# Attention scans: where VectorE takes the sums of weights and their reciprocals in a unit

## The chip, the core and the metric

The kernel runs on one core of a Trainium2 chip. The metric is the device time of one execution in microseconds (us). Five engines work side by side: PE (TensorE, with its weight loads listed apart as PEld), DVE (VectorE), ACT (ScalarE), POOL (GpSimd) and SP (SyncE, which here only issues transfers). Each executes its own list of instructions in order; they meet on semaphores.

## The reference, cut to what matters

The program is two transformer blocks one behind the other. The second has two attention branches, and those hold the change. Both have 8 query heads of width 64 over 2 key/value heads; 1024 rows of queries are worked in 8 blocks of 128. The window branch lets a query block see its own block of keys, the two beside it and 256 context keys; the grid branch lets it see all 1024 keys and the 256 context keys:

```python
def grid_attention(q, k, v, kc, vc):
    b, L, hq, dh = q.shape
    nb = L // BLK
    k_all = jnp.concatenate([k, kc], axis=1)
    v_all = jnp.concatenate([v, vc], axis=1)
    qb = jnp.moveaxis(q.reshape(b, nb, BLK, hq, dh), 1, 0)
    ob = lax.map(lambda qi: dense_attention(qi, k_all, v_all, None), qb)
    return jnp.moveaxis(ob, 0, 1).reshape(b, L, hq * dh)
```

For each row of queries this is: scores, their maximum m, the weights exp(score - m), the sum of the weights, weights times values, and that divided by the sum. The window branch puts a "sink" logit into the maximum and the sum.

## The kernel before, in words

**Tiling.** The class `AttGroup` holds one key/value head of one branch with its 4 query heads; there are four of them, run one after the other: at10 and at11 (window branch), at20 and at21 (grid branch). After the projections of a group comes its scan. A scan has 16 units; a unit is one block n of 128 queries and two heads x0 and x0+1 (`self.units`, n from 0 to 7, x0 0 and 2).

**What one unit takes.** PE multiplies queries and keys into PSUM banks 0 to 3 (`scores`: two pieces a head in the window branch, three in the grid branch). DVE takes the maximum of each piece, joins them and negates (`scores` in `dve`, "neg"; in the window branch it first adds the masks `wm` to the bank). ACT makes the exponentials of a head (tile P) and their sum per piece into columns 4 to 6 of the small tile `sm` (`soft` in `act`). DVE adds the three columns into column 8 and takes the reciprocal there (`soft` in `dve`: one "sum" and one "rs" a head). PE transposes P by blocks of 128 keys, two blocks of both heads into one bank, 4 or 5 alternating (`turn`; called a block pair below: 2 or 3 of them a unit in the window branch, 5 in the grid branch). ACT copies the bank into Ph, DVE subtracts to get the rest Pl (`turn` in `dve`), PE multiplies values by Ph and Pl into bank 6 (`av`). Ahead of the first product of a unit PE spreads the two reciprocals of column 8 over bank 6 with two matmuls each (`bank<-cst,at20sm`). At the end (`fin`) ACT copies half of bank 6 to `rsx`, DVE adds the halves and multiplies by the reciprocals into `y`.

**What sets the order.** Every engine walks the same list, `walk`, and does its own part of each step. Step j of unit u does the block pair j of u (`turn`), two steps later its product (`av`), behind the last one `fin`; and between them it does the steps of the next unit, from `first`:

```python
if self.win:
    return [lambda: scores(n, x0), lambda: scores(n, x0 + 1), lambda: soft(n, x0), lambda: soft(n, x0 + 1)]
return [lambda: scores(n, x0), None, lambda: soft(n, x0), lambda: scores(n, x0 + 1), None, lambda: soft(n, x0 + 1)]
```

So in the grid branch DVE's list within one unit is, with a dash for the next unit's work: Pl of pair 0, -maxima of head x0, Pl of pairs 1 and 2, -sum and reciprocal of head x0, Pl of pair 3, -maxima of head x0+1, Pl of pair 4, -sum and reciprocal of head x0+1, `fin`. In the window branch: Pl 0, -maxima x0, Pl 1, -maxima x0+1, Pl 2, -both sums and reciprocals, `fin`. For the very first unit of a scan, `first` runs without a unit ahead of it. PE also has matmuls of another product in its list, `bank<-h,wslot`, the gate of the branch, one of its 8 steps at a time at fixed steps of units 0 to 11 (grid) or 0 to 13 (window) (`gate_pe`); ACT copies each finished gate tile out to `sq` at the end of every second unit (`gate_act`).

Waits go by semaphores that count up; a wait that an engine has already passed is not issued again (`Eng.wait_ge`).

## Time and profile before

| | us |
|---|---|
| median of 3 runs | 4696.1 (4693.6 to 4708.62) |
| the profiled execution | 4691.44, its span 4689.6 |
| scan of at10, first to last sum | 2802.8 to 2933.1 of the span |
| scan of at11 | 3000.7 to 3131.1 |
| scan of at20 | 3289.4 to 3479.0 |
| scan of at21 | 3573.9 to 3762.2 |

The profile gives the busy time of each engine and, for every instruction, start, duration and what ended the idle time ahead of it. The chain of waits is followed back from the last instruction of the program: what stands in it is what sets the time. The four scans take about 640 of the 4690 us; nothing outside them is touched. Line numbers in the rows are those of helpers: L193 and L196 are PE's matmul and transpose, L202 ACT's activation, L205 DVE's and POOL's tensor_tensor, L208 tensor_scalar, L223 the maximum, L226 the sum, L217 the reciprocal. Tiles tell the instructions apart.

### The profile page before, as it was taken

The numbers are of one execution on the slowest core, as the hardware profiler recorded it, in microseconds if no ns is written. First come the engines' busy times: TensorE is split into PE (matmuls) and PEld (weight loads), VectorE is DVE, ScalarE is ACT, GpSimd is POOL, SyncE is SP. The second block draws the span as 40 slices with busy tenths as digits, with TensorE's granted clock in tenths as the row PEclk, the third lists the DMA queues.
The fourth block names the chain that finished last, engine by engine and source line by source line (L and its number), as shares of the span: only waits on it lengthen the run. The fifth ranks groups of instructions, "written<-read, shape, count | busy, mean of one in ns | idle before, by whom it ended". The sixth has DMA issues, their size and how long they took to land.

```text
span 4689.6 us, 46418 instructions
## 1 busy us (share of the span) xinstructions
PE 4275.1 (91%) x18566; PEld 3109.3 (66%) x18566; DVE 2383.8 (51%) x3800; ACT 1547.6 (33%) x2988; POOL 903.6 (19%) x695
## 2 busy tenths in 40 slices
PE   7896889998999999988889999989888998999997
PEld 3455754757788888645457866565665677888886
DVE  2778864153556663336362337564667754333334
ACT  3465631122211111332332215352554633222222
POOL 2112224121334441016161000001000021000001
PEclk9998899999999999897979999999999999999999
DMA  5112243112333441211111211021000031111111
GB/s 193 41 61 86 77 132 110 32 45 81 90 108 113 121 117 48 107 55 45 54 45 54 77 35 39 17 66 47 24 25 19 19 117 36 54 45 53 42 41 63
DMA packets 257800, 308.90 MB, mean 66 GB/s; under 512 B 19072, under 2 KB 209936, under 8 KB 256304
## 3 DMA queue, kind: packets, MB, share of 16 engines
q1 hardware_dynamic: 238096, 227.15, 15.8%
q0 software_dynamic: 17408, 75.64, 5.2%
q8 instruction: 146, 2.39, 0.2%
q10 hardware_dynamic: 2080, 3.15, 0.2%
q14 instruction: 70, 0.57, 0.0%
HBM read 271.61 MB, written 34.28 MB: 65 GB/s over the span
## 4 chain that ended last, share of the span: by engine, by line
PE 61%; DVE 10%; ACT 5%; issue 1%; POOL 1%; DMA 1%; POOLq 0%; DVEq 0%; ACTq 0%
PE bank L193 60%; PE bank L196 2%; DVE Mx L205 1%; ACT Mx L202 1%; ACT at21P L202 1%; ACT at20P L202 1%; POOL sq L205 1%; DVE at21sm L223 1%; DVE at20sm L223 1%; DVE x L211 0%; DMA wslot<-in_w_in 0%; DVE wfl L205 0%; DVE at11sm L223 0%; DVE at21Pl L205 0%; DVE at10sm L223 0%
## 5 line engine op out<-in xcount | busy, mean ns | idle before, releaser
L193 PE MATMUL bank<-h,wslot 128*128 128x512 f32 (+2 forms) x1616 | 691.5, 566 | 32.9 <-DMA wslot<-in_w_in 19.1
L193 PE MATMUL bank<-hT,wslot 128*128 128x512 f32 (+3 forms) x1136 | 462.4, 564 | 17.1 <-DVE hT L211 7.3
L193 PEld LDWEIGHTS bank<-h,wslot 128*128 128x128 f32 (+1 forms) x1616 | 292.0, 191 | 262.7 <-issue 245.6
L193 PEld LDWEIGHTS bank<-hT,wslot 128*128 128x128 f32 (+1 forms) x1136 | 212.4, 190 | 242.8 <-issue 237.8
L193 PE MATMUL bank<-ffn1h,wfh 128*128 128x512 f32 x704 | 279.8, 397 | 11.7 <-DVE ffn1l L211 10.9
L211 DVE SCALAR_TENSOR_TENSOR x<-bank,mod,x 128x512 f32<-128x512 f32 x224 | 164.4, 746 | 245.1 <-PE bank L193 244.8
L193 PE MATMUL bank<-ffn2h,wgh 128*128 128x512 f32 x704 | 276.5, 393 | 9.7 <-DVE ffn2l L211 9.2
L193 PE MATMUL bank<-ffn1l,wfh 128*128 128x512 f32 x704 | 275.0, 391 | 0.0
L193 PE MATMUL bank<-ffn2l,wgh 128*128 128x512 f32 x704 | 274.9, 390 | 0.0
L193 PE MATMUL bank<-ffn2h,wgl 128*128 128x512 f32 x704 | 274.7, 390 | 0.0
L193 PE MATMUL bank<-ffn1h,wfl 128*128 128x512 f32 x704 | 274.5, 390 | 0.0
L205 DVE TENSOR_TENSOR wfl<-wslot,wfh 128x1024 fp32r<-128x1024 f32 (+2 forms) x92 | 152.6, 1659 | 148.3 <-ACT wfh L202 148.3
L205 POOL TENSOR_TENSOR ffn2al<-ffn2ga,ffn2ah 128x512 fp32r<-128x512 f32 x44 | 57.4, 1304 | 655.3 <-ACT ffn2ah L202 655.3
L226 DVE TENSOR_REDUCE at2a<-ffn1t 128x128 f32<-128x1024 f32 x72 | 143.1, 1988 | 45.6 <-POOL ffn1t L205 45.6
L205 POOL TENSOR_TENSOR sq<-sq 128x512 f32<-128x512 f32 (+1 forms) x77 | 94.8, 1231 | 362.9 <-ACT sq L202 358.7
L193 PEld LDWEIGHTS bank<-ffn1h,wfh 128*128 128x128 f32 x704 | 132.6, 188 | 44.5 <-DVE ffn1l L211 10.6
L193 PEld LDWEIGHTS bank<-ffn2h,wgh 128*128 128x128 f32 x704 | 132.6, 188 | 43.2 <-DVE ffn2l L211 10.2
L211 DVE SCALAR_TENSOR_TENSOR ffn2ga<-ffn2gw,par,ffn2ga 128x1024 f32<-128x1024 f32 x44 | 56.5, 1285 | 199.6 <-ACT ffn2ga L202 198.8
L193 PEld LDWEIGHTS bank<-ffn2h,wgl 128*128 128x128 f32 x704 | 132.8, 189 | 27.7
L193 PEld LDWEIGHTS bank<-ffn1h,wfl 128*128 128x128 f32 x704 | 132.6, 188 | 27.9
L193 PEld LDWEIGHTS bank<-ffn2l,wgh 128*128 128x128 f32 x704 | 132.8, 189 | 26.7
L193 PEld LDWEIGHTS bank<-ffn1l,wfh 128*128 128x128 f32 x704 | 132.8, 189 | 25.4
(573 smaller groups left out, 9502.7 us busy)
## 6 DMA issues: line engine op xcount, KB each, us to landing
wslot<-in_w_in SPq DMA_DIRECT2D x40, 1024.0 KB, 5.7
ffn1t<-in_w_mod POOLq DMA_DIRECT2D x64, 512.0 KB, 4.9
wslot<-in_w_ffn_in SPq DMA_DIRECT2D x44, 512.0 KB, 5.4
Mx<-acsT SPq DMA_DIRECT2D x32, 512.0 KB, 4.9
at1w<-in_ada_w POOLq DMA_DIRECT2D x24, 512.0 KB, 4.7
wslot<-in_ffn_w_gate SPq DMA_DIRECT2D x22, 512.0 KB, 4.0
wslot<-in_ffn_w_up SPq DMA_DIRECT2D x22, 512.0 KB, 5.3
wslot<-in_w_ffn_out SPq DMA_DIRECT2D x20, 512.0 KB, 5.3
```

What stands on the lines that cost most here:

```text
L193: return Counted() if counting[0] else self.q.matmul(o, l, r, start=start, stop=stop)
L196: return Counted() if counting[0] else self.q.transpose(o, i, ident)
L202: return Counted() if counting[0] else self.q.activation(o, i, f, **k)
L205: return Counted() if counting[0] else self.q.tensor_tensor(o, a, b, op)
L211: return Counted() if counting[0] else self.q.scalar_tensor_tensor(o, a, s, b, op0, op1)
L223: return Counted() if counting[0] else self.q.reduce_max(o, a, AX.X)
L226: return Counted() if counting[0] else self.q.reduce_sum(o, a, AX.X)
```

## The change

`soft` in `dve` is taken out of the walk (it becomes a step that does nothing), and a new function `sums(u)` does both heads of a unit at once. It is called from `turn`, behind the Pl of pair 0 of the same unit: that is one step later than before for every unit but the first, on the other side of the `fin` of the unit ahead. Both sums stand first, then both reciprocals.

```diff
-            def soft(n, x):
-                s_ = self.sm[n, x]
-                e.wait_ge(*st.act.after("p", n, x))
-                e.reduce_sum(s_[:, 8:9], s_[:, 4:7]).then_inc(d("sum", n, x), 1)
-                e.wait_ge(*d.now())
-                e.reciprocal(s_[:, 8:9], s_[:, 8:9]).then_inc(d("rs", n, x), 1)
+            def sums(u):
+
+                n, x0 = u
+                for x in (x0, x0 + 1):
+                    s_ = self.sm[n, x]
+                    e.wait_ge(*st.act.after("p", n, x))
+                    e.reduce_sum(s_[:, 8:9], s_[:, 4:7]).then_inc(d("sum", n, x), 1)
+                for x in (x0, x0 + 1):
+                    s_ = self.sm[n, x]
+                    e.wait_ge(*d.after("sum", n, x))
+                    e.reciprocal(s_[:, 8:9], s_[:, 8:9]).then_inc(d("rs", n, x), 1)
...
                 self.bt.give((u, i), d.now())
+                if i == 0:
+                    sums(u)
...
-            self.walk(scores, soft, turn, lambda u, i: None, fin, lambda i, j: None)
+            self.walk(scores, lambda n, x: None, turn, lambda u, i: None, fin, lambda i, j: None)
```

DVE's list in the scan of at20, one unit from the middle. Pl is the rest of a block pair, sm0 and sm1 the small tiles of the two heads of the coming unit, sm2 that of the unit behind it. Before, from the Pl of pair 2 on:

```order
L205 TENSOR_TENSOR at20Pl1<-bank5,at20Ph1 128x512
L226 TENSOR_REDUCE at20sm0<-at20sm0 128x1
L217 RECIPROCAL at20sm0<-at20sm0 128x1
L205 TENSOR_TENSOR at20Pl2<-bank4,at20Ph2 128x512
L223 TENSOR_REDUCE at20sm1<-bank3 128x1
L223 TENSOR_REDUCE at20sm1<-bank0 128x1
L223 TENSOR_REDUCE at20sm1<-bank1 128x1
L208 TENSOR_SCALAR at20sm1<-at20sm1 128x1 x2
L205 TENSOR_TENSOR at20Pl3<-bank5,at20Ph3 128x512
L226 TENSOR_REDUCE at20sm1<-at20sm1 128x1
L217 RECIPROCAL at20sm1<-at20sm1 128x1
L205 TENSOR_TENSOR rsx<-bank6,rsx 64x256
```

After, from the Pl of pair 4 of the same unit on:

```order
L205 TENSOR_TENSOR at20Pl3<-bank5,at20Ph3 128x512
L205 TENSOR_TENSOR rsx<-bank6,rsx 64x256
L205 TENSOR_TENSOR y2<-rsx,bank6 64x128 x2
L205 TENSOR_TENSOR at20Pl0<-bank4,at20Ph0 128x512
L226 TENSOR_REDUCE at20sm0<-at20sm0 128x1
L226 TENSOR_REDUCE at20sm1<-at20sm1 128x1
L217 RECIPROCAL at20sm0<-at20sm0 128x1
L217 RECIPROCAL at20sm1<-at20sm1 128x1
L223 TENSOR_REDUCE at20sm2<-bank2 128x1
```

The four small instructions have left the places behind Pl of pair 2 and of pair 4, and stand between Pl of pair 0 of the next unit and the first maximum of the unit behind that.

DVE's list in the scan of at10, the difference at one unit (- is before, + is after; wm is the mask, added to the bank ahead of its maximum):

```order
-L226 TENSOR_REDUCE at10sm4<-at10sm4 128x1
-L217 RECIPROCAL at10sm4<-at10sm4 128x1
-L226 TENSOR_REDUCE at10sm5<-at10sm5 128x1
-L217 RECIPROCAL at10sm5<-at10sm5 128x1
 L205 TENSOR_TENSOR rsx<-bank6,rsx 64x256
 L205 TENSOR_TENSOR y1<-rsx,bank6 64x128 x2
 L205 TENSOR_TENSOR at10Pl0<-bank4,at10Ph0 128x512
+L226 TENSOR_REDUCE at10sm4<-at10sm4 128x1
+L226 TENSOR_REDUCE at10sm5<-at10sm5 128x1
+L217 RECIPROCAL at10sm4<-at10sm4 128x1
+L217 RECIPROCAL at10sm5<-at10sm5 128x1
```

Here they move from ahead of `fin` to behind the first Pl. The lists of PE, ACT, POOL and SP keep their order.

## Rows read from the trace of the kernel before

**Rows 1.** The page, chain that ended last, shares of the span by engine.

```profile
PE 61%; DVE 10%; ACT 5%; issue 1%; POOL 1%; DMA 1%; POOLq 0%; DVEq 0%; ACTq 0%
```

**Rows 2.** Stretches, at10 and at20: us, busy PE PEld DVE ACT POOL, clock, DMA, GB/s.

```profile
2795.00:2940.00 145.00, 123.91 (x617) 84.31 (x617) 103.29 (x342) 75.35 (x231) 0.00 (x0) 0.94 0.11 33
...
3275.00:3490.00 215.00, 182.48 (x997) 136.72 (x995) 144.62 (x358) 118.04 (x298) 1.26 (x1) 0.93 0.07 22
```

**Rows 3.** Waits, 3275 to 3490: who for whom, us in total, times, longest.

```profile
DVE at20sm L226 <- ACT at20P L202: 38.2, 32, 3.3
```

**Rows 4.** Instructions of L226 and L217: duration ns min/median/max, first and last start.

```profile
L226 DVE TENSOR_REDUCE at20sm<-at20sm x32: 155/156/158, 3289.4 to 3479.0; 128x1 f32<-128x3 f32 x32
```

```profile
L217 DVE RECIPROCAL at20sm<-at20sm x32: 162/163/166, 3289.6 to 3479.2; 128x1 f32<-128x1 f32 x32
```

**Rows 5.** Timeline, grid branch, around a first head's sum: start us, us, engine.

```profile
3391.00 0.60 ACT L202 ACTIVATE at20Ph<-bank 128x512 fp32r<-128x512 f32 x1
...
3391.15 0.16 DVE L226 TENSOR_REDUCE at20sm<-at20sm 128x1 f32<-128x3 f32 x1 [0.77 <-ACT at20P L202]
...
3391.34 0.16 DVE L217 RECIPROCAL at20sm<-at20sm 128x1 f32<-128x1 f32 x1
...
3391.64 0.69 DVE L205 TENSOR_TENSOR at20Pl<-bank,at20Ph 128x512 fp32r<-128x512 f32 x1
```

**Rows 6.** Timeline, window branch, behind a second head's sum, up to `fin`.

```profile
2885.86 0.38 ACT L202 ACTIVATE rsx<-bank 64x256 f32<-64x256 f32 x1
...
2886.06 0.16 DVE L217 RECIPROCAL at10sm<-at10sm 128x1 f32<-128x1 f32 x1
...
2886.28 0.42 DVE L205 TENSOR_TENSOR rsx<-bank,rsx 64x256 f32<-64x256 f32 x1
```

**Rows 7.** Timeline, opening of the scan of at20, PE and DVE.

```profile
3289.51 0.42 PE L193 MATMUL bank<-at20kl,at20qs 128*128 128x256 f32 x1
3289.58 0.16 DVE L217 RECIPROCAL at20sm<-at20sm 128x1 f32<-128x1 f32 x1
3289.66 1.60 DVE L223 TENSOR_REDUCE at20sm<-bank 128x1 f32<-128x512 f32 x3
```

**Rows 8.** Chain of waits, window branch, two units: start us, us, what.

```profile
2887.53 0.69 DVE at10Pl L205
...
2892.70 1.12 ACT at10P L202 x4
2893.96 0.63 PE bank L196 x4
...
2903.78 0.69 DVE at10Pl L205
```

**Rows 9.** Timeline, window branch, PE at the transposes that the chain passes by.

```profile
2885.95 0.14 PEld L196 LDWEIGHTS bank<-cst,at10P 128*128 128x128 f32 x1 [0.35 <-ACT at10P L202]
2886.26 0.60 PE L196 MATMUL bank<-cst,at10P 128*128 128x128 f32 x4
```

**Rows 10.** Chain of waits, grid branch, from a Pl of pair 0 on.

```profile
3398.29 0.69 DVE at20Pl L205
...
3401.66 0.66 PE bank L196 x4
```

**Rows 11.** Timeline, grid branch, the other unit: its "neg" and ACT's exponentials.

```profile
3388.72 0.46 DVE L208 TENSOR_SCALAR at20sm<-at20sm 128x1 f32<-128x1 f32 x2
...
3389.22 0.68 ACT L202 ACTIVATE at20P<-bank,at20sm 128x512 f32<-128x512 f32 x1
```

**Rows 12.** Timeline, grid branch, PE behind the load of gate weights in mid-scan.

```profile
3349.72 1.97 PE L193 MATMUL bank<-h,wslot 128*128 128x512 f32 x2 [4.39 <-DMA wslot<-in_w_in]
```

**Rows 13.** Timeline, window branch, last unit of the scan of at10.

```profile
2934.74 0.69 DVE L205 TENSOR_TENSOR at10Pl<-bank,at10Ph 128x512 fp32r<-128x512 f32 x1 [0.23 <-ACT at10Ph L202]
2934.86 1.12 PE L193 MATMUL bank<-cst,at10sm 128*64 128x128 f32 x4
```

**Rows 14.** A stretch of at20 behind the gate's units; columns as in rows 2.

```profile
3455.90:3461.00 5.10, 5.10 (x26) 4.38 (x26) 4.52 (x13) 2.32 (x5) 0.00 (x0) 0.69 0.00 0
```

## The prediction

> **What bounds the kernel now.** I read the chain of waits first, by engine [rows 1]: PE holds 61% of the span, DVE 10%, ACT 5%. The change touches nothing but DVE's list in the four attention scans, about 640 of 4690 us, so I then read the stretches of those scans [rows 2]. PE is busy 124 of 145 us in one and 182 of 215 in the other, at a mean granted clock of 0.94 and 0.93; DVE 103 and 145 us. No engine is full: a scan is a loop of dependences that passes from engine to engine, and the question is which DVE instructions stand in that loop. The waits [rows 3] make the change look worth a lot: in one grid scan DVE stands 38.2 us in front of the sums, 32 times, until ACT has written the last exponentials. But a wait counts only where what stands behind it on DVE could have gone earlier.
>
> **Part 1: what is taken away from behind the maxima.** 32 sums of 0.155 us and 32 reciprocals of 0.163 us a scan [rows 4], 64 pairs in the window scans and 64 in the grid scans. Take the first head of a grid unit [rows 5]: sum at 3391.15, reciprocal 0.19 later at 3391.34, over at 3391.50. Behind it stands the Pl of pair 3, and that needs ACT's Ph, which stands behind the same exponentials on ACT: 3391.00 to 3391.60. Pl starts at 3391.64, by the Ph and not by the reciprocal. Worth nothing, and the wait in front of the sum only changes its name: DVE will now stand as long in front of Pl. The second head is the same with `fin` behind it [rows 6]: ACT's copy `rsx` stands behind the exponentials and ends at 2886.24, the reciprocal at 2886.22, the add starts at 2886.28. Worth 0.02 us at most. Where the odd unit has ACT copy a gate tile first, the copy comes later still and the cover is wider. So the removal gives 0 in steady state, and the cover is ACT's own next instruction.
>
> One place is different: the opening of a grid scan, where no unit runs ahead. There the sum of the first head holds back the maxima of the second: they start at 3289.66, 0.08 after the reciprocal at 3289.58, all three in 1.60 us [rows 7]. Without it the first of them could run while ACT works, and the other two as PE delivers: its last score matmul runs from 3289.51 to 3289.93, so the second piece is there by 3289.51. Second and third maximum, 768 of the 1280 columns and so three fifths of the 1.60, 0.96 us, would end near 3290.5, where the three ended at 3291.26: 0.7 us earlier. The first transposes wait for this, so **-0.7 us in each of two grid scans, -1.4**. The window scans do both maxima ahead of the sums already: 0.
>
> **Part 2: what is put in behind the first Pl.** Four small instructions between Pl of pair 0 and the next maximum. No wait comes with them in front of the sums (the transposes of pair 0 needed both heads' exponentials already); each reciprocal waits for its sum. The price of one place: a DVE instruction that needs nothing starts 0.08 after the start of a small one ahead of it (reciprocal 3289.58, maximum 3289.66 [rows 7]); one that needs the result of its predecessor starts 0.19 after it [rows 5]. So sum, sum at 0.08, reciprocal at 0.19, reciprocal at 0.27, next maximum at 0.35: **0.35 us**. Bounds: four times 0.07 to 0.08 is 0.3 if nothing had to be waited for; the sum of the durations, 2 x 0.155 + 2 x 0.163 = 0.64, if nothing overlapped. I take 0.35, since both spacings are read from these very instructions.
>
> The Trainium skill, page "VectorE: DVE Perf Modes", section "The DRAIN you can't avoid", says that the next operation does not start until the pipeline is empty. The maximum that starts 0.08 after the start of a reciprocal of 0.16 [rows 7] speaks against it; by that rule a place costs 0.64. It is a rival below.
>
> **Part 3: how many of these places stand in the loop.** *Window branch.* The chain goes Pl of pair 0 (2887.53), masks, maxima, Pl 1, masks, maxima, ACT's exponentials (2892.70), transposes of the next unit (2893.96) [rows 8], then stays on PE through the whole next unit, and comes back to a Pl of pair 0 at 2903.78. So every second place is on it in full: 7 of 16, and the last one ahead of the unit without gate steps too, 8 x 0.35 = 2.8 us a scan. In the unit that the chain passes by, PE's first weight load waits for ACT at 2885.95, its transposes start at 2886.26 behind the gate product [rows 9]; a load leads its matmul by 0.03 where nothing is queued, so there is 0.28 of slack and a place costs 0.35 - 0.28 = 0.07: 5 times, 0.35 us. Two places are free: behind the opening, where the chain runs on PE, and ahead of the load of gate weights in mid-scan. Last, the final unit: PE's spread of the reciprocals starts at 2934.86, right behind the `fin` of the unit ahead, while Pl of pair 0 runs 2934.74 to 2935.43 [rows 13]. Now the reciprocals come only behind that Pl. A free instruction follows a large one about 0.09 before its end: sums from 2935.34, second reciprocal from 2935.61, over at 2935.77. With no maxima and no gate product in front of it PE waits for it: first spread at about 2935.7 instead of 2934.86, **+0.84**. A window scan: 2.8 + 0.35 + 0.84 = 4.0, two of them 8.0 us.
>
> *Grid branch.* The loop is two units again. In the one the chain goes Pl of pair 0 (3398.29), maxima, "neg", Pl of pair 1, transposes of pair 3 (3401.66) [rows 10], since these need the bank that Pl 1 frees: in full. In the other the chain comes over PE and ACT to the exponentials of the first head at 3389.22, but DVE's "neg" for them is over at 3388.72 + 0.46 = 3389.18 [rows 11], and 0.04 is what a semaphore takes here (Pl 0.04 behind Ph in [rows 5]): slack 0, in full too. Of 15 places (the last unit has no maxima behind it) one is hidden in the opening, and one where PE stands 4.39 us for gate weights [rows 12], during which DVE catches up. 13 x 0.35 = 4.55 a scan, 9.1 us for two. In the last grid unit PE's spread comes behind transposes that wait for Pl of pair 0 anyway: 0.
>
> **Sum.** 8.0 + 9.1 - 1.4 = **+15.7 us**. The profiled execution took 4691.4 (span 4689.6), which would become 4707.1; the median of the three runs is 4696.1, 4.7 above it, and I predict for the median: 4711.8. With a place at 0.3 the 42 full ones (16 window, 26 grid) give 12.6, the ten half-hidden ones 0.2, the two window ends some 1.5, less 1.4: +12.9. At 0.64 it is 26.9 + 3.6 + 2.3 - 1.4 = +31.4.
>
> **Rivals.**
> *A good part of the places is covered.* "Slack 0" in one kind of grid unit rests on two instants 0.04 apart, and a shift of Ph against "neg" that the first delay itself brings could free the second. If those 6 places a grid scan fall out (12 x 0.35 = 4.2), and the half-hidden ones and the window ends too (0.7 + 1.7), +9.1 is left: 4705.2. For it: bounds that close tend to hide a little slack between them. Against: DVE's start in that unit follows PE, so both shift together.
> *No overlap on DVE.* The place costs 0.64: +31.4, 4727.5. Against it the 0.08 [rows 7]; for it that no row shows two sums or two reciprocals in a row. This is the rule of the Trainium skill named above.
> *The clock.* PE idles 0.35 us more per unit. Behind the gate's units the granted clock is 0.69 over 5.1 us [rows 14], a part of it at the lower of the two levels (1.2 against 2.4 GHz), right behind waits of PE for Pl and for P. 5.1 us at 0.69 instead of 1.00 is 1.6 us lost; three such more a scan are +19, in all 4731. The gate product, which keeps PE busy in 12 or 14 units of 16, speaks against it.
> *Faster.* The removed pairs cost DVE 0.27 each (0.19 + 0.08), 0.54 a unit. If the release of Pl 3 and of `fin` were by DVE and not by ACT, and the four instructions found room behind Pl 0 because "neg" were early, the about 60 units would give back 0.54 each, -32 us: 4664. This decides itself at one point: whether the reciprocal ends behind ACT's copy. It ends 0.10 before Ph [rows 5] and 0.02 before `rsx` [rows 6], so I see it only where ACT is quicker than shown.
>
> **How the numbers follow.** Chance of the forecast 0.62, of the covered places 0.20, of no overlap 0.08, of the clock 0.06, of faster 0.04. A difference of under 0.3%, 14.1 us, can hardly be told from none here, and the forecast stands just over it: of its 0.62 I put 0.38 above and 0.24 below. Slower 0.38 + 0.08 + 0.06 = 0.52, within 0.3% 0.24 + 0.20 = 0.44, faster 0.04. The range: the forecast by the bounds of the place is +12.9 to +31.4, the covered places give +9; with some 2 us either way for the runs it is 4701 to 4728.
>
> **What would show it.** Right: behind each first Pl four small rows 0.08, 0.19 and 0.27 after the first, the maximum at 0.35; the waits in front of L226 gone, waits of Pl for Ph and of `fin` for `rsx` longer by about as much, no less time between exponentials and Pl 3; a pair of grid units 0.7 us longer, a pair of window units 0.42 longer than 16.25 [rows 8]; PE waiting for DVE's reciprocals once at the end of a window scan; second maxima of the grid opening 0.7 us earlier. Wrong: a pair of grid units longer by 0.35 only, or the small rows 0.16 apart, or a lower clock in the loop.

## The result, and the profile after

The changed kernel takes 4712.79 us (median of 10 runs, 4707.69 to 4717.64) against 4692.66 us for the kernel before (10 runs, 4689.92 to 4708.62). The ratio is 1.0042, with a 95% interval of 1.0033 to 1.0051: slower by 15.5 to 24 us, 20.1 between the medians. The prediction said +15.7 us and 4711.8. Of the two, +15.7 is the one to judge: that 4711.8 lies within 1 us of the measured 4712.79 is luck, since the base of 4696.1 was the median of three runs and 3.4 above that of ten, and the change was forecast 4.4 too small. One run in eleven of the version "grid branch only" below took 8666.03 us; it is left out of every comparison.

The page of the changed kernel, busy time by engine (us, share of the span, instructions), and then the chain that ended last, by engine:

```profile
PE 4284.3 (91%) x18566; PEld 3111.7 (66%) x18566; DVE 2368.0 (50%) x3800; ACT 1550.5 (33%) x2988; POOL 906.7 (19%) x695
...
PE 58%; DVE 12%; ACT 5%; POOL 2%; issue 1%; DMA 1%; POOLq 0%; DVEq 0%; ACTq 0%; SPq 0%
```

Against [rows 1] the chain has passed from PE (61% to 58%) to DVE (10% to 12%). These shares say only in which direction to look. The stretches of the scans of at10 and at20, with the columns of [rows 2] (length, busy PE, PEld, DVE, ACT, POOL, granted clock, DMA, GB/s):

```profile
2799.00:2951.00 152.00, 127.91 (x618) 85.53 (x617) 100.20 (x344) 76.27 (x231) 0.00 (x0) 0.93 0.10 32
...
3300.00:3514.00 214.00, 183.08 (x999) 137.99 (x1000) 134.78 (x353) 116.99 (x295) 0.00 (x0) 0.93 0.07 22
```

The windows are not cut at the same instants as in [rows 2], so their lengths are not to be compared, and the one of before holds a few more DVE instructions of the preparation. DVE's busy time has fallen from 144.6 to 134.8 us in the grid scan, about half of it by these few and the other half because small instructions that stood in separate pairs now overlap (32 sums and 32 reciprocals of about 0.16 alone are 10.2 us, 16 places of 0.32 are 5.1). So the busy time falls while the time rises: what costs here is the order, not the amount of work. To compare lengths I take an anchor that exists in every kernel, from the first maximum of a scan to its last `y`. In the profiled executions that is 140.1, 139.0, 206.5 and 205.3 us for at10, at11, at20 and at21 before, together 690.9; after, 145.6, 143.8, 210.6 and 208.8, together 708.9. So **18.0 us came in inside the four scans**. The two profiled executions are 26.2 us apart (the one of after, at 4717.64, is the longest of its ten). Of that, 5.3 lie ahead of the first scan, where no instruction has moved, 2.2 between at10 and at11, and 0.7 behind the last. The 5.3 say nothing about the change: in a second profile of the kernel before the first scan starts at 2792.3 us, in the first at 2798.9. The 2.2 are taken up below.

Where does DVE wait now? The waits in the scan of at20, columns as in [rows 3] (who for whom, us in total, times, longest):

```profile
DVE at20Pl L205 <- ACT at20Ph L202: 37.0, 28, 4.7
DVE rsx L205 <- ACT rsx L202: 32.3, 16, 2.3
```

The same two rows of the kernel before, over the stretch of [rows 3]:

```profile
DVE at20Pl L205 <- ACT at20Ph L202: 15.1, 15, 4.9
...
DVE rsx L205 <- ACT rsx L202: 6.3, 13, 1.0
```

The 38.2 us in front of L226 [rows 3] have no row any more. In their place the waits of Pl for Ph grew by 21.9 and those of `fin` for `rsx` by 26.0, together 47.9. Removing the largest wait of DVE bought nothing: it took another name and grew by what the small instructions no longer filled. The small instructions are all still there, 32 of each a scan.

Now the place itself. Timeline of the changed kernel in the scan of at20 (start us, us, engine, what; in brackets the wait ahead of it). A row with x2 or x3 is a group of instructions and its time is from the start of the first to the end of the last:

```profile
3455.81 0.69 DVE L205 TENSOR_TENSOR at20Pl<-bank,at20Ph 128x512 fp32r<-128x512 f32 x1 [0.47 <-ACT at20Ph L202]
...
3456.42 0.21 DVE L226 TENSOR_REDUCE at20sm<-at20sm 128x1 f32<-128x3 f32 x2
3456.60 0.23 DVE L217 RECIPROCAL at20sm<-at20sm 128x1 f32<-128x1 f32 x2
3456.74 1.60 DVE L223 TENSOR_REDUCE at20sm<-bank 128x1 f32<-128x512 f32 x3
...
3458.88 0.69 ACT L202 ACTIVATE at20P<-bank,at20sm 128x512 f32<-128x512 f32 x1 [0.20 <-DVE at20sm L208]
```

Pl, then the first sum at 0, the first reciprocal at 0.18, the maximum at 0.32. From the lengths of the x2 groups (0.21 for two of 0.146, 0.23 for two of 0.156) the second sum stands at 0.07 and the second reciprocal at 0.07 to 0.08 behind the first. The last row is what makes it expensive: ACT had been idle for 0.20 us before the exponentials and was let go by DVE's "neg", in the very kind of unit in which the prediction called the slack 0.

What a place costs, in each of the two kinds of unit, shows best in the times of `y`. First the kernel before, then the one after, three successive units in the scan of at20 (the timeline of DVE):

```profile
3421.53 0.59 DVE L205 TENSOR_TENSOR y<-rsx,bank 64x128 f32<-64x128 f32 x2
...
3433.14 0.59 DVE L205 TENSOR_TENSOR y<-rsx,bank 64x128 f32<-64x128 f32 x2
...
3445.40 0.59 DVE L205 TENSOR_TENSOR y<-rsx,bank 64x128 f32<-64x128 f32 x2
```

```profile
3430.23 0.59 DVE L205 TENSOR_TENSOR y<-rsx,bank 64x128 f32<-64x128 f32 x2
...
3442.81 0.59 DVE L205 TENSOR_TENSOR y<-rsx,bank 64x128 f32<-64x128 f32 x2
...
3454.75 0.59 DVE L205 TENSOR_TENSOR y<-rsx,bank 64x128 f32<-64x128 f32 x2
```

Before, steps of 11.61 and 12.26; after, 11.94 (3442.81 to 3454.75) and 12.58. **Each kind of unit is 0.32 to 0.33 longer, the full price of a place in both.** The window branch, three units in the scan of at10, before and then after:

```profile
2878.94 0.59 DVE L205 TENSOR_TENSOR y<-rsx,bank 64x128 f32<-64x128 f32 x2
...
2886.73 0.59 DVE L205 TENSOR_TENSOR y<-rsx,bank 64x128 f32<-64x128 f32 x2
2887.53 0.69 DVE L205 TENSOR_TENSOR at10Pl<-bank,at10Ph 128x512 fp32r<-128x512 f32 x1 [0.21 <-ACT at10Ph L202]
...
2895.19 0.59 DVE L205 TENSOR_TENSOR y<-rsx,bank 64x128 f32<-64x128 f32 x2
```

```profile
2886.77 0.59 DVE L205 TENSOR_TENSOR y<-rsx,bank 64x128 f32<-64x128 f32 x2
...
2894.88 0.59 DVE L205 TENSOR_TENSOR y<-rsx,bank 64x128 f32<-64x128 f32 x2
2895.50 0.69 DVE L205 TENSOR_TENSOR at10Pl<-bank,at10Ph 128x512 fp32r<-128x512 f32 x1
...
2903.47 0.59 DVE L205 TENSOR_TENSOR y<-rsx,bank 64x128 f32<-64x128 f32 x2
```

Steps of 7.79 and 8.46 became 8.11 and 8.59: +0.32 in the one kind of unit, +0.13 to 0.14 in the other. The rows of Pl show where the other 0.18 went: before, DVE stood idle for 0.21 us between `y` and Pl of pair 0, waiting for Ph; after, Pl follows the end of `y` in 0.03.

The end of a window scan is the place where PE meets the reciprocals. Timeline of the changed kernel in the last unit of at10, to be read against [rows 13]:

```profile
2944.08 0.69 DVE L205 TENSOR_TENSOR at10Pl<-bank,at10Ph 128x512 fp32r<-128x512 f32 x1
...
2944.69 0.21 DVE L226 TENSOR_REDUCE at10sm<-at10sm 128x1 f32<-128x3 f32 x2
2944.87 0.23 DVE L217 RECIPROCAL at10sm<-at10sm 128x1 f32<-128x1 f32 x2
...
2945.18 1.08 PE L193 MATMUL bank<-cst,at10sm 128*64 128x128 f32 x4 [1.40 <-DVE at10sm L217]
```

PE's spread of the reciprocals began 0.12 us behind the start of Pl of pair 0 in [rows 13]. Now it begins 1.10 behind it, with a named wait of 1.40 us for L217. One unit earlier the same wait stands once more, with 0.95 us, but that step (7.02 to 7.34) grew by no more than in the kernel of the section "The place alone", where PE does not wait for reciprocals.

And the opening of the grid scan, PE and DVE, against [rows 7]:

```profile
3303.79 0.68 DVE L223 TENSOR_REDUCE at20sm<-bank 128x1 f32<-128x512 f32 x1
...
3307.33 0.41 PE L193 MATMUL bank<-at20kl,at20qs 128*128 128x256 f32 x1
3307.36 1.02 DVE L223 TENSOR_REDUCE at20sm<-bank 128x1 f32<-128x512 f32 x2 [2.89 <-PE bank L193]
```

The first maximum of the second head now runs 3.6 us ahead of the other two, and these start with PE's last score matmul and take 1.02 instead of 1.60. First maximum to first Pl is 11.12 and 10.62 us in the two grid scans, where it was 11.80 and 11.81. The 0.7 is the one gain of the change, and it is as predicted. The other 0.5 of the second scan does not repeat (a second profile of the changed kernel has 11.12 twice) and goes with a higher granted clock: 0.80 from the first maximum to the first `y`, 0.71 in the kernel before.

### The profile page after: what moved, and what is told of

It reads as the page before. It is cut to its first block, busy times and chain, and to the rows that moved or that the text cites. A ratio compares the mean times of both kernels' runs of the same rounds, so it can differ in the third digit from the quotient of the medians.

```text
span 4715.8 us, 46424 instructions
## 1 busy us (share of the span) xinstructions
PE 4284.3 (91%) x18566; PEld 3111.7 (66%) x18566; DVE 2368.0 (50%) x3800; ACT 1550.5 (33%) x2988; POOL 906.7 (19%) x695
## 3 DMA queue, kind: packets, MB, share of 16 engines
q1 hardware_dynamic: 238096, 227.15, 15.7%
## 4 chain that ended last, share of the span: by engine, by line
PE 58%; DVE 12%; ACT 5%; POOL 2%; issue 1%; DMA 1%; POOLq 0%; DVEq 0%; ACTq 0%; SPq 0%
PE bank L193 57%; PE bank L196 1%; DVE Mx L205 1%; ACT at21P L202 1%; ACT at20P L202 1%; DVE at20sm L223 1%; DVE at21sm L223 1%; ACT Mx L202 1%; POOL sq L205 1%; DVE y L205 0%; DVE x L211 0%; DVE at11sm L223 0%; DVE wfl L205 0%; DMA wslot<-in_w_in 0%; DVE at10sm L223 0%
## 5 line engine op out<-in xcount | busy, mean ns | idle before, releaser
L193 PE MATMUL bank<-ffn1h,wfh 128*128 128x512 f32 x704 | 279.9, 398 | 11.7 <-DVE ffn1l L211 10.8
L193 PE MATMUL bank<-ffn2h,wgh 128*128 128x512 f32 x704 | 276.2, 392 | 10.2 <-DVE ffn2l L211 9.6
L226 DVE TENSOR_REDUCE at2a<-ffn1t 128x128 f32<-128x1024 f32 x72 | 143.1, 1987 | 47.7 <-POOL ffn1t L205 47.7
L193 PEld LDWEIGHTS bank<-ffn2h,wgh 128*128 128x128 f32 x704 | 132.4, 188 | 43.9 <-DVE ffn2l L211 10.8
```

Source lines behind the costliest of these rows:

```text
L193: return Counted() if counting[0] else self.q.matmul(o, l, r, start=start, stop=stop)
L226: return Counted() if counting[0] else self.q.reduce_sum(o, a, AX.X)
```

## The experiments

Two theories stood against each other after the result. **The place:** the 18 us come from the four small instructions behind Pl of pair 0, whatever they compute, and nothing came back for their leaving. **The late results:** they come from sums and reciprocals being ready later, for PE. Beside these: is the place 0.33 because of overlap on DVE, and why 20 us rather than 15.7? Each version's median is compared with that of the kernel before timed beside it: 4695.85 for the first four below, 4694.22 for the next four, 4694.41 for the last two. "Scans" is the sum of the four lengths as above, from one profile. A ratio is not the quotient of the two medians; the two can differ by some 3 us.

### Without sums and reciprocals

Leaves out the division by the sum of the weights: PE spreads the column of the negated maximum instead of that of the reciprocal, and DVE does neither sums nor reciprocals.

```diff
-                        e.wait_ge(*st.dve.after("rs", n, x0 + x))
-                        e.matmul(..., self.sm[n, x0 + x][:, 8:9].to_broadcast([128, 64]), ident)...
+                        e.wait_ge(*st.dve.after("neg", n, x0 + x))
+                        e.matmul(..., self.sm[n, x0 + x][:, 3:4].to_broadcast([128, 64]), ident)...
...
-            self.walk(scores, soft, turn, ...)
+            self.walk(scores, lambda n, x: None, turn, ...)
```

> Takes all 128 sums of weights and 128 reciprocals out of the four scans and puts nothing in their place; PE spreads the column with the negated maximum instead of the reciprocal, so the scans leave the division by the sum out. Theory 'the place' (the removed pairs stood behind ACT's next instruction and were worth nothing; what costs is where the four instructions now stand): the kernel before less only the 0.7 us of each grid opening, -1 to -2 us. Rival 'the pairs were on the path': they were worth up to 0.54 us a unit, -10 to -32 us, and the new place costs that much more.

Measured 4689.55 us against 4695.85, ratio 0.9994 (0.9985 to 1.0003): between 7 us less and 1.4 us more, so the medians' -6.3 stands at the edge of it. Scans 692.3 against 690.9, and all steps of the loop are as before (12.26 and 11.60, 8.45 and 7.79). The cover is seen in the timeline of this kernel, ACT and DVE around the place where a first head's sum used to be:

```profile
3407.26 0.60 ACT L202 ACTIVATE at20Ph<-bank 128x512 fp32r<-128x512 f32 x1
...
3407.90 0.69 DVE L205 TENSOR_TENSOR at20Pl<-bank,at20Ph 128x512 fp32r<-128x512 f32 x1 [1.26 <-ACT at20Ph L202]
```

Ph starts, and 0.64 behind that start comes Pl, exactly as in [rows 5] (3391.00 and 3391.64) where sum and reciprocal stood between. Taking the pairs away altogether, the most that any move out of this position can give, is worth nothing in the steps; a gain of 10 us or more is excluded. That is Part 1 of the prediction, shown by its removal. What remains, -0.7 in each grid opening, was here too: first maximum to first Pl 11.11 and 11.12.

### The place alone

The kernel before with four spare instructions of the same size behind Pl of pair 0, whose result nobody reads:

```diff
+            def spare(u):
+                n, x0 = u
+                for x in (x0, x0 + 1):
+                    e.reduce_sum(self.sm[n, x][:, 9:10], self.sm[n, x][:, 4:7]).then_inc(d("sum9", n, x), 1)
+                for x in (x0, x0 + 1):
+                    e.wait_ge(*d.after("sum9", n, x))
+                    e.reciprocal(self.sm[n, x][:, 9:10], self.sm[n, x][:, 9:10]).then_inc(d("rs9", n, x), 1)
...
+                if i == 0:
+                    spare(u)
```

> The kernel before, with its sums and reciprocals where they were, and two more sums and two more reciprocals into an unused column of the small tile, at the place where the change puts them (behind Pl of pair 0). Theory 'the place': the same loss as the change less its gain at the grid openings and without the late reciprocals at the window ends (1.2 us each): about 20 + 1.4 - 2.4, +19 us. Rival 'late results': if what costs is that PE gets the reciprocals late, these spare instructions, for which nobody waits, cost clearly less than the change, under +10.

4709.82 us, ratio 1.0035 (1.0021 to 1.0048): +14.0 between the medians, +17.3 in the scans, where +19 was expected and under +10 by the rival. Scans 708.2, where after has 708.9. That the two sums are so close is partly chance: the window scans are 285.4 us here and 289.4 there, the grid scans 422.8 and 419.5. The steps are the better witness. The steps are those of the changed kernel: `y` in at20 at

```profile
3430.17 0.59 DVE L205 TENSOR_TENSOR y<-rsx,bank 64x128 f32<-64x128 f32 x2
3442.10 0.59 DVE L205 TENSOR_TENSOR y<-rsx,bank 64x128 f32<-64x128 f32 x2
3454.68 0.59 DVE L205 TENSOR_TENSOR y<-rsx,bank 64x128 f32<-64x128 f32 x2
```

that is 11.93 and 12.58, and in the window branch 8.10 and 8.59. No result is late here, no sum has been moved, and every step of the loop has its loss. This decides between the two theories for the steady state: it is the place. What the late results add is seen at the end of a window scan only, where PE of this kernel does not wait:

```profile
2935.57 1.12 PE L193 MATMUL bank<-cst,at10sm 128*64 128x128 f32 x4
```

From the last `y` but one to the last `y` of at10 this kernel takes 4.99, the changed one 5.71, before 4.50. So the end costs 1.2 in all, 0.5 of it by the place and 0.7 by the late reciprocals. This interval too has longer forms: 5.15 in one of four of the kernel before, 6.09 and 6.11 in later versions.

### The place twice

The changed kernel with the same four spare instructions behind its own:

```diff
                 if i == 0:
                     sums(u)
+                    spare(u)
```

> The changed kernel with the four instructions of the place twice (the second time into an unused column). Theory 'the place': another 0.35 us or somewhat less at each of the 42 places in the loop, the 0.28 of slack in the ten others now used up so that they cost in full as well: 52 x 0.33 to 0.35, +17 to +18 over the changed kernel, about +37 to +38 over the one before. Rival 'slack used up only once or clock': over +25 on top of the changed kernel if longer waits of PE bring its clock down again and again.

4723.51 us, ratio 1.0064 (1.0051 to 1.0077), 13.7 above the kernel with one spare place. Scans 722.4, 13.5 above after. The steps in at20 are 12.89 and 12.25, another 0.31 in each. The window branch is the telling one, its three rows in at10:

```profile
2881.86 0.59 DVE L205 TENSOR_TENSOR y<-rsx,bank 64x128 f32<-64x128 f32 x2
2890.28 0.59 DVE L205 TENSOR_TENSOR y<-rsx,bank 64x128 f32<-64x128 f32 x2
2899.18 0.59 DVE L205 TENSOR_TENSOR y<-rsx,bank 64x128 f32<-64x128 f32 x2
```

8.42 and 8.90: the kind of unit that took the first place for 0.14 takes the second for 0.31, in full. So there was a slack, it was 0.32 - 0.14 = 0.18 us, and the first place has used it up. Slack is a thing that one delay consumes. The total came out lower than expected: +37 to +38 over the kernel before was forecast, measured are +27.7 between the medians (+24 to +36 by the ratio's interval) and +31.5 in the scans. The steps grew nearly as forecast, 13 a scan by 0.31 (0.33 to 0.35 was said), which is 4.0; but the four scans grew by 3.7, 2.9, 3.4 and 3.4 over the changed kernel. The missing part lies in the openings, the steps with the load and the ends, which come in different lengths from profile to profile (below).

### The kernel before once more

The same text as the kernel before, to see how far profiles of one program differ.

> The kernel before, once more, for a second profile of it. The changed kernel's scans measured 18.0 us longer and the stretch between the two window scans 2.2 us longer, at a granted clock of 0.96 instead of 1.00. If that 2.2 is the luck of one execution, stretches outside the scans differ by about as much between these two profiles of one and the same kernel; if it comes with the change, they agree within 0.3 us.

4695.14 us, ratio 0.9998 (0.9989 to 1.0007). Scans 691.4 against 690.9, but a single scan differs by up to 1.2 (at11 140.2 against 139.0, at20 205.5 against 206.5), so the 0.5 of the sum is a lucky figure. Steps of the loop repeat within 0.02. The last interval of the window scans was 4.44 and 5.15. Outside the scans the two profiles do differ, the start of the first scan by 6.6 us. But the stretch between the two window scans, which the expectation was about, was 59.0 both times.

### Window branch only, grid branch only

The changed kernel with the old `soft` for one branch and `sums` for the other:

```diff
+            def soft(n, x):
+                if self.win:
+                    return
...
-                if i == 0:
+                if i == 0 and self.win:
                     sums(u)
```

> The change in the two window scans alone; the grid scans keep their sums behind the maxima. Theory 'the place', by the steps measured in the changed kernel (0.32 and 0.14 us in turn, 1.2 at the end, half of it luck of the clock): 4.5 us in each window scan, +9 in all; grid scans as before, the stretch around the load of gate weights in mid-scan 17.0 us. Rival 'clock': the grid's load stretch is longer here too.

> The change in the two grid scans alone. Theory 'the place': 13 x 0.32 less 0.7 at the opening is +3.5 a scan. Theory 'clock after the load': the stretch with the load of gate weights takes 18 us or more instead of 17.0, as in five of the six grid scans with the four instructions in that place, because TensorE's clock stays at the lower level for longer; then +4.5 a scan, +9 in all. If it takes 17.0 here, the longer stretch was luck.

Window only: 4703.1 us, ratio 1.0022 (1.0012 to 1.0031), +8.9. Grid only: 4703.2 without the run of 8666.03, ratio 1.0018 (1.0009 to 1.0027), +9.0. Window only is as expected (+9), grid only lies at the +9 of the clock theory and 2 above the +7 of the other. The two together are 17.9 against the 20.1 of the whole change: within the intervals they add up, and each branch carries about half. In the traces the scans are 698.8 and 699.2, +7.9 and +8.3 over before, and each branch that kept its order kept its steps (12.27 and 11.61 in the grid branch of the first). The grid's step with the load of gate weights took 17.07 and 16.90 us in the first kernel, 16.95 and 18.06 in the second: one scan of each kind, so neither theory is decided by it.

### Serial in the place

Sum, reciprocal, sum, reciprocal, each behind its predecessor's end:

```diff
                     e.reduce_sum(s_[:, 8:9], s_[:, 4:7]).then_inc(d("sum", n, x), 1)
-                for x in (x0, x0 + 1):
-                    s_ = self.sm[n, x]
-                    e.wait_ge(*d.after("sum", n, x))
+                    e.wait_ge(*d.now())
                     e.reciprocal(s_[:, 8:9], s_[:, 8:9]).then_inc(d("rs", n, x), 1)
```

> The changed kernel with the four instructions of the place in the order sum, reciprocal, sum, reciprocal. If the price of a place is the dependence (0.18 from a sum to its reciprocal) and not the number of instructions, it now is 2 x (0.18 + 0.08) = 0.52 instead of 0.33: the steps of 11.93 us in the grid scans become 12.12, and the kernel is 52 x 0.19 = +10 us over the changed one, +30 over the one before. If four instructions cost the same in any order, the steps stay at 11.93.

4720.43 us, ratio 1.0059 (1.0046 to 1.0072): +26.2 between the medians where +30 was expected; scans 719.7, which is 10.8 above after. The place in at20:

```profile
3347.99 0.15 DVE L226 TENSOR_REDUCE at20sm<-at20sm 128x1 f32<-128x3 f32 x1
3348.17 0.16 DVE L217 RECIPROCAL at20sm<-at20sm 128x1 f32<-128x1 f32 x1
3348.25 0.14 DVE L226 TENSOR_REDUCE at20sm<-at20sm 128x1 f32<-128x3 f32 x1
3348.42 0.16 DVE L217 RECIPROCAL at20sm<-at20sm 128x1 f32<-128x1 f32 x1
3348.50 1.60 DVE L223 TENSOR_REDUCE at20sm<-bank 128x1 f32<-128x512 f32 x3
```

The rows show both spacings: a reciprocal 0.17 or 0.18 behind the start of the sum that it reads, and the next, unrelated instruction 0.08 behind the start of the reciprocal. The place is 0.51 long. All steps of the loop grow by it: 12.77 and 12.12 in the grid branch, 8.79 and 8.30 in the window branch, about 0.19 above after in each. What the prediction feared as "no overlap" is half there with the four in this order, and it costs some 10 us in the scans.

### One sum and one reciprocal for both heads

The six small tiles lie side by side in one, and one instruction takes both heads:

```diff
-            self.sm = Ring([sb(f"{nm}sm{i}", [16]) for i in range(6)])
+            self.smt = sb(f"{nm}sm", [96])
+            self.sm = Ring([self.smt[:, i * 16:i * 16 + 16] for i in range(6)])
...
+                two = self.smt[:, i * 16:i * 16 + 32].rearrange("p (x c) -> p x c", c=16)
+                e.reduce_sum(two[:, :, 8:9], two[:, :, 4:7]).then_inc(d("sum", n, x0 + 1), 1)
+                e.wait_ge(*d.now())
+                e.reciprocal(two[:, :, 8:9], two[:, :, 8:9]).then_inc(d("rs", n, x0 + 1), 1)
```

> The changed kernel with the small tiles of the two heads side by side in one tile, so that one sum (128x2 from 128x2x3) and one reciprocal do both heads: two instructions in the place instead of four. By the same spacings 0.18 + 0.08 = 0.26 instead of 0.33 a place: steps of 11.86 us in the grid, 52 x 0.07 = 3.6 us under the changed kernel, about +16 over the one before. If the price were 0.08 an instruction, it would halve to 0.16, about 9 us under the changed kernel.

4710.42 us, ratio 1.0036 (1.0023 to 1.0048): +16.2, as expected; scans 706.7, 2.2 below after. The place:

```profile
3346.95 0.15 DVE L226 TENSOR_REDUCE at20sm<-at20sm 128x2 f32<-128x6 f32 x1
3347.14 0.17 DVE L217 RECIPROCAL at20sm<-at20sm 128x2 f32<-128x2 f32 x1
3347.22 1.60 DVE L223 TENSOR_REDUCE at20sm<-bank 128x1 f32<-128x512 f32 x3
```

0.27 instead of 0.32. Half the instructions save only 0.05, because the two that went were the cheap, overlapped ones. The pair that depends on each other is what the place costs. Between 0.27 (this), 0.32 (after) and 0.51 (serial) the scans go 706.7, 708.9, 719.7. By the sum of the prediction's 52 places (42 full and ten whose slack is gone by then) serial should be 52 x 0.19 = 9.9 above after, and this 52 x 0.05 = 2.6 below; measured 10.8 and 2.2. That fits the count of the places; the steps, each longer by 0.19 in the one and shorter by 0.05 to 0.06 in the other, show it more surely, since single parts of a scan vary by 1 us and more.

### The opening only

The kernel before, with only the first unit of each grid scan late:

```diff
             def soft(n, x):
+                if not self.win and (n, x // 2 * 2) == self.units[0]:
+                    return
...
+                if i == 0 and not self.win and u == self.units[0]:
+                    sums(u)
```

> The kernel before, with only the first unit of each grid scan doing its sums behind its first Pl, where the maxima behind them are covered by PE; all other units as before. By the steps: first maximum to first Pl 11.12 instead of 11.81 us in both grid scans, all later steps as before, -1.4 us in all, 0.03%, below what the times can tell. It is the version that the steps point to. Rival: the first place costs something too, and nothing is left of the 1.4.

4692.47 us, ratio 1.0000 (0.9991 to 1.0009). First maximum to first Pl went from 11.80 and 11.81 to 10.77 and 10.63, a gain of 1.0 and 1.2 in the trace; the scans are 689.3 against 690.9. In the run times 1 or 2 us cannot be told from nothing, and part of the gain in the trace goes with the granted clock of these openings, 0.81 and 0.80 instead of 0.70 and 0.71. It is the only part of the change that the traces show to gain anything, and no version that I ran is measurably faster than the kernel before.

### The changed kernel once more

> The changed kernel once more, for a second profile and in the same call as the one above. The steps repeat within 0.02 us (11.93 and 12.58 in the grid, 8.11 and 8.60 in the window); the time is 18 to 20 us over the one before. What differs from profile to profile without a change of the kernel (openings, the stretch around the load, the ends, the stretch behind the first window scan) differs again by up to 1 to 3 us each. If the longer load stretch comes with the change, it is 18 us or so here in at least one of the two grid scans.

4716.01 us, ratio 1.0048 (1.0034 to 1.0062): +21.6, where 18 to 20 was expected; scans 709.4 against 708.9. The steps repeat (12.58 and 11.92 to 11.94, 8.60 and 8.11). The step with the load is 16.77 in at20 and 17.94 in at21.

## Why the prediction was right, step by step

**The removal is worth nothing: right.** Without the sums and reciprocals at all the kernel takes the same time (0.9985 to 1.0003), and Pl starts 0.64 behind the start of Ph with or without them.

**The opening: right up to the first Pl**, 0.7 us (11.80 to 11.12); 1.2 in the second grid scan, 0.5 of which goes with the clock. Behind the first Pl some of it is gone again (the table below).

**The price of a place: nearly right.** Predicted sums at 0 and 0.08, reciprocals at 0.19 and 0.27, the maximum at 0.35. Measured 0, 0.07, 0.18, about 0.25, 0.32 to 0.33. The sums are 0.146 us long here where they were 0.155. On 42 full places that is -1 us. The rival of no overlap (0.64) has fallen: the maximum starts 0.14 behind the start of reciprocals that together take 0.23. The Trainium skill, page "VectorE: DVE Perf Modes", section "The DRAIN you can't avoid", says in one sentence that the next operation does not start until the pipeline is empty, and at the end of the same paragraph that one that is not held starts earlier. The prediction quoted the first sentence alone. The rows here agree with the second.

**Every grid place in full: right for the steps of the loop**, and this was the weakest step of the prediction. It is not so for the step with the load and for the last one (below). The covered places, the rival with a chance of 0.20, would have left one kind of grid unit unchanged; both got 0.32 to 0.33 longer, and the second place added 0.31 to both again. The "slack 0" that was read from two instants 0.04 apart was real.

**The half-hidden window place: the size was off, because a second path was overlooked.** A step costs 0.13 to 0.14 and not 0.07. The slack of 0.28 in front of the transposes [rows 9] was there. They start 0.85 us behind the start of the gate product ahead of them before (2885.41 and 2886.26) and 0.87 behind it after (2893.26 and 2894.13), while the distance from the weight load to them shrinks from 0.31 to 0.03. But the place also delays ACT's copy `rsx`, with it `fin`, and `fin` stands ahead of the next Pl of pair 0 on DVE. There the slack is smaller: the 0.21 of idle time ahead of Pl in the rows above, less the 0.03 that is left when nothing is waited for, is 0.18, and 0.32 - 0.18 = 0.14. The same 0.18 fits the other two prices: of 0.27 (joined) 0.08 to 0.09 is paid in this kind of step, of 0.51 (serial) 0.33. Ten times 0.07 is +0.7 us. The pair of window units is 0.45 longer, where 0.42 was said.

**The end of the window scans: the mechanism was right, the size was off.** PE waits for L217, and the step comes to 1.2 and not 0.84, +0.8 in two scans. The place itself costs 0.5 there, as the kernel with spare instructions shows, and 0.3 of this is between Pl of pair 0 and Pl of pair 1 of the last unit, a place that the prediction did not count; the late reciprocals cost 0.7. PE waits at the last two units, not only at the last.

**What is left.** The account can be checked part by part. From the mean of two profiles of the changed kernel less the mean of two of the kernel before, both scans of a branch together (us):

| part | window: predicted | measured | grid: predicted | measured |
|---|---|---|---|---|
| first maximum to first `y` | 0 | +1.0 | -1.4 | -0.9 |
| places in full (16 and 26) | +5.6 | +5.2 | +9.1 | +8.5 |
| half-hidden places (10) | +0.7 | +1.5 | | |
| step with the load of gate weights | 0 | +0.2 | 0 | +1.7 |
| last step | +1.7 | +2.1 | 0 | -1.3 |
| sum | +8.0 | +10.0 | +7.7 | +8.0 |

The grid branch came out right partly because two parts that the prediction put at nothing nearly cancel. In the window branch +1.0 comes from an opening of at10 that is 13.8 to 14.0 us in seven profiles and 14.8 to 15.1 in five; the kernel without sums, which has nothing in the place, is among the five, so this is not shown to be the change's. The two grid parts go with the granted clock. In the step with the load in the middle [rows 12] the prediction said that the place is hidden. PE of the changed kernel, behind that load in at20:

```profile
3368.17 2.05 PE L193 MATMUL bank<-h,wslot 128*128 128x512 f32 x2 [4.46 <-DMA wslot<-in_w_in]
```

The wait is that of [rows 12], but what follows differs. Stretches of some 7 us behind the load, columns as above, of the kernel before, of the changed one, and of the kernel with the opening only, which has no place there at all:

```profile
3349.70:3357.00 7.30, 7.28 (x31) 4.92 (x32) 2.52 (x6) 2.88 (x8) 0.00 (x0) 0.77 0.00 1
```

```profile
3368.10:3375.50 7.40, 7.33 (x27) 5.39 (x28) 1.40 (x3) 2.99 (x8) 0.00 (x0) 0.58 0.00 1
```

```profile
3344.70:3352.00 7.30, 7.23 (x27) 5.28 (x28) 1.62 (x5) 2.99 (x8) 0.00 (x0) 0.59 0.00 1
```

Of the two levels, 2.4 and 1.2 GHz, a granted clock of 0.58 is mostly the lower one. With 0.77 the step takes about 17.0 us, with 0.58 or 0.59 about 18 (17.5 to 18.8). Where the step is short the place is hidden in it, as predicted (16.77 in the changed kernel's second profile). But it was long in 10 of the 14 grid scans with the place, and in 1 of 10 without. **That the change makes the long form more frequent is likely by the counts, not shown**: the kernel with the opening only has it without a place there.

The last step of a grid scan goes the other way. In at20, before and then after:

```profile
3479.89:3489.70 9.81, 8.00 (x40) 6.52 (x38) 4.44 (x9) 3.30 (x6) 0.00 (x0) 0.67 0.00 0
```

```profile
3502.59:3511.64 9.05, 6.87 (x39) 5.49 (x37) 4.68 (x13) 3.12 (x6) 0.00 (x0) 0.81 0.00 0
```

It took 9.0 to 9.1 us in 8 of the 14 grid scans with the place and 9.6 to 10.1 in the others, and never under 9.7 in the 10 without. In all eight short ones the granted clock is 0.86 to 0.88 in the step ahead of it and 0.81 in it; in all others it is 0.95 to 1.00 and 0.66 to 0.71. The low stretch has moved. The rival of the clock was thus wrong in size and sign (+19 behind the units of the gate, where the last four steps together grew by 0.4 us in the mean), but the clock does take part.

From 18.0 in the scans to 20.1 between the medians is within the interval of the latter (15.5 to 24), and needs no cause. But one part outside the scans is longer in the changed kernel. The stretch between the scans of at10 and at11, before:

```profile
2938.40:2998.00 59.60, 58.01 (x148) 27.41 (x148) 18.76 (x26) 11.15 (x19) 7.61 (x6) 1.00 0.06 19
```

and after:

```profile
2949.20:3011.00 61.80, 60.24 (x148) 29.01 (x148) 18.78 (x27) 11.15 (x19) 7.62 (x6) 0.96 0.06 19
```

The same 148 matmuls take 2.2 us more at a clock of 0.96 than at 1.00. From the end of at10 to the start of at11 the stretch is 59.0 us in both profiles of the kernel before, in those of one spare place, two places, serial order, grid only and opening only; it is 60.7 to 61.9 in both of the changed kernel and in those of window only, joined, and without sums. So it is long in four of the six profiles in which the window branch has the sums in the new place, in none of the five in which it has them in the old one, and in the one without sums. That it comes with the change is possible and not shown; so part of the 20.1 may be this.

The range as the prediction states it, 4701 to 4728, is also not quite what its working gives: 4696.1 with 9.1 less 2 and with 31.4 plus 2 is 4703 to 4730.

## What to carry to other kernels

Removing a wait of an engine gained something only where the next instruction on that engine was ready before the wait ended. Read what stands behind the wait and what releases it: here ACT's next instruction covered both small ones, 38 us of waits a scan were worth 0, and their cheapest place was inside the wait. In a loop that passes through every engine, an instruction put in front of "the next maximum" cost its start-to-start time, 0.07 to 0.08 us if it was independent and 0.18 if it read its predecessor's result, less any slack, multiplied by the number of units. Slack has to be looked for on every path that the delay takes: here 0.28 on PE's was of no use, because the one over ACT's copy and `fin` had 0.18. To test such a reading, put the same instructions there a second time and take them away altogether: these two runs tell the price, the cover and the slack apart. Compare a prediction with the measurement part by part, too: a sum can be right because two parts cancel.

## What the runs showed of the hardware

- DVE starts an independent small instruction 0.07 to 0.08 us behind the start of one that is 0.15 to 0.16 long, and a dependent one, through a semaphore, 0.17 to 0.19 behind. Four in the order sum, sum, reciprocal, reciprocal take 0.32 to 0.33, alternating 0.51, and two of double width (128x2) 0.27.
- One program's parts come in two lengths according to where stretches of low granted clock fall: 17.0 or 18 us for the step behind a load of weights (clock 0.77 or 0.58), 9.8 or 9.05 for the last step of a grid scan (0.67 or 0.81), 59.0 or 61 to 62 from one window scan to the next (1.00 or 0.94 to 0.97). A part that the change does not touch can differ by 2 us between two profiles, so the steps of a loop, repeated dozens of times, are a better witness than the difference of two spans.
